# The first down product of a gated ConvFFN starts behind the last up product without a barrier between the two stages (fp32 two-layer backbone, one core)

## The reference, cut to what matters

```python
def conv_ffn(h, w_up, conv_w, conv_b, w_down):
    u = h @ w_up
    up = jnp.pad(u, ((0, 0), (1, 1), (0, 0)))
    u = up[:, :-2] * conv_w[0] + up[:, 1:-1] * conv_w[1] + up[:, 2:] * conv_w[2] + conv_b
    a, b = jnp.split(u, 2, axis=-1)
    return (jax.nn.gelu(a) * b) @ w_down

def post_add(x, y, g, gate):
    return x + gate * rms_norm(y, g)
```

## Time and profile before

| | |
|---|---|
| median of 3 runs | 1652.82 us |
| profiled execution, its own time | 1657.06 us |
| span of the profiled execution | 1655.3 us |
| PE busy in the span | 1518.8 us, 92% |
| DVE, ACT, POOL busy | 968.6, 728.8, 596.9 us |
| mean granted clock of PE | 0.97 |
| up stage's last product ends, down products start, layer 0 | 752.8, 760.1 us |
| the same, layer 1 | 1526.2, 1531.1 us |

### The profile page before, as it was taken

One profiled execution on the slowest core, in us unless ns is written; L12 is line 12 of the kernel. 1 busy time (PEld: TensorE's weight loads), 2 busy tenths in 40 slices (PEclk: granted clock), 3 DMA queues, 4 the chain that ended last, 5 costly groups with the idle time before them and its releaser, 6 DMA issues.

```text
span 1655.3 us, 22238 instructions
## 1 busy us (share of the span) xinstructions
PE 1518.8 (92%) x7560; PEld 1216.7 (74%) x7560; DVE 968.6 (59%) x1465; ACT 728.8 (44%) x1240; POOL 596.9 (36%) x529
## 2 busy tenths in 40 slices
PE   6889798889999999998999698889988899999998
PEld 1777466667888888886888577677776688887886
DVE  2448577557678666833334566688775544444455
ACT  3432466535323333323353445377774544443453
POOL 1342244233222222322333531364442444443454
PEclk9999799999999999999999899899999899999999
DMA  8120750104355344411122112010001233332232
GB/s 329 47 84 13 248 188 25 51 1 132 123 178 153 115 126 140 127 39 39 63 66 63 53 52 80 25 50 1 1 1 51 77 102 89 101 98 67 83 96 101
DMA packets 129135, 143.85 MB, mean 87 GB/s; under 512 B 7160, under 2 KB 95484, under 8 KB 129064
## 3 DMA queue, kind: packets, MB, share of 16 engines
q1 hardware_dynamic: 129064, 142.91, 27.6%
HBM read 140.79 MB, written 2.10 MB: 86 GB/s over the span
## 4 chain that ended last, share of the span: by engine, by line
PE 79%; DVE 8%; ACT 5%; POOL 3%; issue 2%; DMA 2%; SPq 0%; POOLq 0%; DVEq 0%; ACTq 0%
PE ps L462 22%; PE ps L463 22%; PE ps L464 22%; PE ps L1400 3%; PE ps L1386 2%; PE ps L1411 1%; ACT pT_hi L1451 1%; DVE hT_lo L781 1%; DVE hT_hi L779 1%; ACT prob L1440 1%; DMA start_w<-in_ada_w_dram 1%; PE ps L1413 1%; PE ps L666 1%; DVE o_tmp L1516 1%; DMA ada_w<-in_ada_w_dram 1%
## 5 line engine op out<-in xcount | busy, mean ns | idle before, releaser
L454 POOL TENSOR_TENSOR w_lo<-raw,w_hi 128x1024 fp32r<-128x1024 f32 (+1 forms) x184 | 348.0, 1893 | 644.9 <-ACT w_hi L447 644.9
L462 PE MATMUL ps<-hT_hi,w_hi 128*128 128x512 f32 (+1 forms) x1072 | 383.6, 358 | 7.3 <-DVE hT_lo L781 6.4
L463 PE MATMUL ps<-hT_lo,w_hi 128*128 128x512 f32 (+1 forms) x1072 | 381.2, 356 | 0.0
L464 PE MATMUL ps<-hT_hi,w_lo 128*128 128x512 f32 (+1 forms) x1072 | 378.8, 353 | 0.0
L447 ACT ACTIVATE w_hi<-raw 128x1024 fp32r<-128x1024 f32 (+1 forms) x200 | 172.9, 866 | 190.4 <-PE ps L464 166.6
L462 PEld LDWEIGHTS ps<-hT_hi,w_hi 128*128 128x128 f32 x1072 | 202.8, 189 | 46.6 <-DVE hT_lo L781 10.0
L464 PEld LDWEIGHTS ps<-hT_hi,w_lo 128*128 128x128 f32 x1072 | 202.0, 188 | 29.7
L463 PEld LDWEIGHTS ps<-hT_lo,w_hi 128*128 128x128 f32 x1072 | 202.7, 189 | 27.8
L2053 DVE TENSOR_TENSOR g_lo<-act_g,g_hi 128x768 fp32r<-128x768 f32 (+1 forms) x84 | 106.7, 1277 | 164.2 <-ACT g_hi L2003 162.9
L462 PE MATMUL ps<-w_hi,g_hi 128*128 128x512 f32 x420 | 166.0, 395 | 3.5 <-DVE g_lo L2053 3.0
L464 PE MATMUL ps<-w_hi,g_lo 128*128 128x512 f32 x420 | 164.0, 390 | 0.0
(11 more groups left out here) (234 smaller groups left out, 2497.0 us busy)
## 6 DMA issues: line engine op xcount, KB each, us to landing
raw<-in_ffn_w_up_dram SPq DMA_DIRECT2D x84, 512.0 KB, 3.9
ada_w_up<-in_ada_w_dram SPq DMA_DIRECT2D x48, 512.0 KB, 4.1
raw<-in_ffn_w_down_dram SPq DMA_DIRECT2D x84, 256.0 KB, 2.6
ada_w<-in_ada_w_dram SPq DMA_DIRECT2D x32, 512.0 KB, 5.0
start_w<-in_ada_w_dram SPq DMA_DIRECT2D x8, 1024.0 KB, 11.4
raw<-in_c_w_qkv_dram SPq DMA_DIRECT2D x12, 512.0 KB, 3.6
raw<-in_ab_w_in_dram SPq DMA_DIRECT2D x8, 512.0 KB, 4.1
raw<-in_ab_w_out_dram SPq DMA_DIRECT2D x8, 512.0 KB, 3.8
```

Source lines behind the costliest of these rows:

```text
L454: by.tensor_tensor(w_lo[:, slot, 0:width], raw[:, n % RAW, 0:width], w_hi[:, slot, 0:width].bitcast(F32), ALU.subtract).then_inc(lo_split, 1)
L462: nc.tensor.matmul(outp, s_hi, m_hi, start=first, stop=False, skip_group_check=True)
L463: nc.tensor.matmul(outp, s_hi, m_lo, start=False, stop=False, skip_group_check=True)
L464: return nc.tensor.matmul(outp, s_lo, m_hi, start=False, stop=last, skip_group_check=True)
```

## The change

The after_phase of the down stage goes from all four engines; the `close` of the up stage stays. The first activation tile is split into the unused fourth slot of `w_hi` and `w_lo` (`first_g`): ACT does it in the last turn behind unit 3, DVE's low part follows behind unit 4. ACT and DVE split tiles 1 and 2 where they split three before. PE's `gate_tensor` for the latent tokens follows the last up unit directly; the tiles of down unit 0 take their activations from the fourth slot, and before tile t of it PE waits for the taps of the up unit whose banks it overwrites (`TURNS * TURN + t // 2 + 1`). DVE's loop over the first half starts one turn later, since its first three are now written out. In layer 0 the condition of the copy into `gate_rows` is worded anew and takes place where it did.

```diff
@@ up_scalar, turn
                     else:
                         split_hi(act, f"down{l}", m - (TURN - 3), BANK, free=False)
+                    if last and m == 3:
+                        down_activation(act, l, nt, 0, 0, first=True)
...
             turn(TURNS - 1, True)
-            for m in range(3):
+            for m in (1, 2):
                 down_activation(act, l, nt, m, 0)
             close(act, "act")
@@ up_vector, turn
+                    if last and m == 4:
+                        down_remainder(dve, l, nt, 0, 0, 0, first=True)
@@ down_tensor
-            after_phase(pe, before)
             gate_tensor(pe, l, tag, 1, (0, 1))
...
+                    if first and not half:
+                        pe.wait_ge(s(f"taps{l}"), TURNS * TURN + t // 2 + 1)
                     tt = slice(t * P, (t + 1) * P)
-                    mm = mm3(bank(t), g_hi[:, slot, tt], g_lo[:, slot, tt], w_hi[:, slot, 0:BANK],
+                    gh, gl = first_g() if first and not half else (g_hi[:, slot, :], g_lo[:, slot, :])
+                    mm = mm3(bank(t), gh[:, tt], gl[:, tt], w_hi[:, slot, 0:BANK],
                              w_lo[:, slot, 0:BANK], first, last)
@@
+        def first_g():
+
+            return w_hi[:, 3, 0:TOK], w_lo[:, 3, 0:TOK]
+
-        def down_activation(act, l, nt, m, i):
+        def down_activation(act, l, nt, m, i, first=False):
             T = nt * P
-            nc.scalar.activation(g_hi[:, m, 0:T], act_g[:, bass.ds(i * 3 + m, 1), 0:T].rearrange("p a n -> p (a n)"),
+            g = first_g()[0] if first else g_hi[:, m, :]
+            nc.scalar.activation(g[:, 0:T], act_g[:, bass.ds(i * 3 + m, 1), 0:T].rearrange("p a n -> p (a n)"),
                                  ACT.Copy).then_inc(s(f"g_hi{l}"), 1)
@@ down_scalar, down_pool
-            after_phase(act, before)
...
-            after_phase(pool, before)
@@ down_vector
+        def down_remainder(dve, l, nt, half, m, i, first=False):
             T = nt * P
-            after_phase(dve, before)
+            dve.wait_ge(s(f"g_hi{l}"), i * 3 + (half * FT + m + 1))
+            gh, gl = first_g() if first else (g_hi[:, m, :], g_lo[:, m, :])
+            nc.vector.tensor_tensor(gl[:, 0:T], act_g[:, bass.ds(i * 3 + m, 1), 0:T].rearrange("p a n -> p (a n)"),
+                                    gh[:, 0:T].bitcast(F32), ALU.subtract).then_inc(s(f"g_lo{l}"), 1)
...
-            split_activations(0, 0, DTURNS)
+            for m in (1, 2):
+                down_remainder(dve, l, nt, 0, m, 0)
+            split_activations(0, 1, DTURNS)
```

More of the change, by code:

```diff
@@ L1893, in up_vector, with turn @@
             dve.sem_inc(s(f"taps{l}"), 3)
-            def turn(i, with_ada):
+            def turn(i, with_ada, last=False):
                 if with_ada:
@@ L1922, in turn @@
                                                 gelu[:, 0:T], conv_b[:, 0:T], ALU.mult).then_inc(s(f"gated{l}"), 1)
-                    if l == 0 and not with_ada and m == 1:
+                    if last and m == 4:
+                        down_remainder(dve, l, nt, 0, 0, 0, first=True)
+                    if l == 0 and last and m == 1:
                         dve.wait_ge(s("ada_sum"), 8)
@@ L1931, in up_vector @@
                 turn(i, l == 0)
-            turn(TURNS - 1, False)
+            turn(TURNS - 1, False, last=True)
             close(dve, "dve")
@@ L1946, in down_sync, with down_tensor @@
                         load_unit(sp, f"down{l}", half * FT + m, src, BANK, i, 3)
-        def down_tensor(pe, l, before, nt):
+        def down_tensor(pe, l, nt):
             phase, tag = f"down{l}", f"ffnpost{l}"
-            after_phase(pe, before)
             gate_tensor(pe, l, tag, 1, (0, 1))
@@ L1999, in down_split, with down_scalar @@
             down_activation(act, l, nt, m, i)
-        def down_activation(act, l, nt, m, i):
+        def first_g():
+            return w_hi[:, 3, 0:TOK], w_lo[:, 3, 0:TOK]
+        def down_activation(act, l, nt, m, i, first=False):
             T = nt * P
-            nc.scalar.activation(g_hi[:, m, 0:T], act_g[:, bass.ds(i * 3 + m, 1), 0:T].rearrange("p a n -> p (a n)"),
+            g = first_g()[0] if first else g_hi[:, m, :]
+            nc.scalar.activation(g[:, 0:T], act_g[:, bass.ds(i * 3 + m, 1), 0:T].rearrange("p a n -> p (a n)"),
                                  ACT.Copy).then_inc(s(f"g_hi{l}"), 1)
-        def down_scalar(act, l, before, nt):
+        def down_scalar(act, l, nt):
             tag = f"ffnpost{l}"
-            after_phase(act, before)
             for half in range(2):
@@ L2035, in down_scalar, with down_pool @@
             close(act, "act")
-        def down_pool(pool, l, before, nt):
-            after_phase(pool, before)
+        def down_pool(pool, l, nt):
             for half in range(2):
@@ L2044, in down_pool, with down_vector @@
             close(pool, "pool")
-        def down_vector(dve, l, before, nt):
+        def down_remainder(dve, l, nt, half, m, i, first=False):
             T = nt * P
-            after_phase(dve, before)
+            dve.wait_ge(s(f"g_hi{l}"), i * 3 + (half * FT + m + 1))
+            gh, gl = first_g() if first else (g_hi[:, m, :], g_lo[:, m, :])
+            nc.vector.tensor_tensor(gl[:, 0:T], act_g[:, bass.ds(i * 3 + m, 1), 0:T].rearrange("p a n -> p (a n)"),
+                                    gh[:, 0:T].bitcast(F32), ALU.subtract).then_inc(s(f"g_lo{l}"), 1)
+        def down_vector(dve, l, nt):
             def split_activations(half, first, last):
@@ L2051, in split_activations @@
                     for m in range(3):
[L2052 to L2055, removed]
-            split_activations(0, 0, DTURNS)
+                        down_remainder(dve, l, nt, half, m, i)
+            for m in (1, 2):
+                down_remainder(dve, l, nt, 0, m, 0)
+            split_activations(0, 1, DTURNS)
             if l == 0:
@@ L2112, in _ @@
                 up_tensor(pe, l, NT[l])
-                down_tensor(pe, l, b + 8, NT[l])
+                down_tensor(pe, l, NT[l])
         @block.scalar
@@ L2126, in _ @@
                 up_scalar(act, l, b + 7, NT[l])
-                down_scalar(act, l, b + 8, NT[l])
+                down_scalar(act, l, NT[l])
         @block.gpsimd
@@ L2140, in _ @@
                 up_pool(pool, l, b + 7)
-                down_pool(pool, l, b + 8, NT[l])
+                down_pool(pool, l, NT[l])
         @block.vector
@@ L2155, in _ @@
                 up_vector(dve, l, b + 7, NT[l])
-                down_vector(dve, l, b + 8, NT[l])
+                down_vector(dve, l, NT[l])
 def shape_constants():
```

## The result

| | before | changed |
|---|---|---|
| median of 6 runs each | 1652.27 us | 1643.63 us (1642.29 to 1647.71) |
| ratio, 95% interval | | 0.9947 (0.9930 to 0.9965) |
| profiled execution, its own time | 1657.06 us | 1647.71 us |
| step from up to down, layer 0 | 9.47 us | 2.12 us |
| step from up to down, layer 1 | 5.52 us | 2.12 us |

The forecast was 1642.3 us, the range 1639.8 to 1646.6.

The account below looks back on a forecast made before the run. PE, busy 92% of the span, was taken to bound the kernel. Savings of 7.25 (layer 0) and 3.28 (layer 1) sum to 10.53 us; 1652.82 - 10.53 = 1642.3 us, range 1639.8 to 1646.6.

Parts of the forecast that it names:

- PE's step bounds: Up to down, both layers: PE's waits for DVE's drain at the two barriers, 8.1 us in all, lengthen the kernel.
- What stays in the step: Between up and down products after the change: gates 1.72 us plus PE's drain 0.50, sum 2.22 per layer.
- The row of the drain between the halves: Profile row of PE's drain between the halves, used to price the drain left in the step at 0.50 us.
- Layer 0, 7.25 us: Layer 0's step from up to down costs 9.47 us; less the remaining 2.22, the saving is 7.25.
- Layer 1, 3.28 us: Layer 1's step from up to down costs 5.50 us; less the remaining 2.22, the saving is 3.28.
- The operands: First down units: weights, activations and taps arrive before PE needs them, so no stall enters the sum.
- the pessimistic ends: Unit 1's low part, latest start of DVE's subtraction: ready at least 0.41 us early in layer 0, 0.32 in layer 1.
- POOL in DVE's way: Unit 1: POOL's split or the drain delays DVE's subtraction in both layers; 2.6 us less saved, 1644.9; rival, 8%.
- given back: End of layer 0's stage: something paced by loads loses its share again, leaving 3.3 us saved, 1649.5; rival, 4%.
- ring without its lead: Down stages: each of 84 units would wait, at 5.8 us per unit costing some 17, time 1659; rival, 2%.
- stall that the barrier had covered: PE running from stage to stage without rest: idle 2.04 us once per layer, costing 4.1, so 1646.4; rival, 5%.

Follow-up runs that it names:

- two more subtractions: Changed kernel with two useless DVE subtractions between its last product and the low parts of tiles 1 and 2; median 1647.12 us, ratio 0.9961.

## Why the prediction was right

Steps of all ten traces, in us, with the time that each trace's execution took:

| kernel | step, layer 0 | step, layer 1 | between the steps | time |
|---|---|---|---|---|
| before | 9.47 | 5.52 | 763.9 | 1657.06 |
| before, second trace | 8.22 | 7.13 | 759.9 | 1650.13 |
| changed | 2.12 | 2.12 | 764.6 | 1647.71 |
| changed, second trace | 2.12 | 2.13 | 759.8 | 1643.47 |
| barrier in layer 0 | 9.49 | 2.11 | 764.5 | 1654.03 |
| barrier in layer 1 | 2.12 | 7.22 | 759.9 | 1644.63 |
| barrier on PE alone | 8.69 | 7.13 | 760.1 | 1651.89 |
| no early tile | 8.46 | 6.01 | 762.6 | 1654.39 |
| no drain on PE | 1.76 | 1.75 | 765.1 | 1643.70 |
| two more subtractions | 2.11 | 2.13 | 765.9 | 1647.38 |

- **PE's step bounds.** Right, and shown: with only PE held at the barrier the time is that of the kernel before; with the other engines held only where PE is held too, the layers' shares add.
- **What stays in the step.** Forecast 2.22 us, measured 2.12. The gates took 1.76 where I had 1.72, the drain 0.36 where I had 0.50 (the last from the kernel without it). The row of the drain between the halves was the right one to take; it was 0.14 too dear.
- **Layer 0, 7.25 us.** Measured 7.35 between the two first traces, 6.1 between the second ones, since the clock came back sooner in that trace of the kernel before. It fell in all four traces with a barrier here, and the step cost 8.2 to 9.5.
- **Layer 1, 3.28 us.** Measured 3.40 between the first traces and 5.0 between the second. This term was too small for three of the four traces with a barrier here: I took the granted clock of 1.00 behind the wait for the rule. In the three other traces it fell and the step cost 7.1 to 7.2. How often each happens, four traces don't say.
- **The operands.** Right that nothing waits. The margins were 0.70 and 0.61 us, of which DVE can use 0.57 and 0.47, and not the 0.41 and 0.32 of the pessimistic ends: the 0.60 us ahead of DVE's subtractions was nearly all barrier. DVE starts them 0.13 us behind its product, its drain included. The prediction's two ends were themselves 0.06 too large: it divided merged rows by three, 0.90 and 0.63, where one subtraction by itself takes 0.96 and 0.69.
- **POOL in DVE's way.** It was not, for units 1 and 2: POOL's split of unit 3 began at 760.48 in layer 0, behind both subtractions (757.91 + 1.83 = 759.74). In layer 1 the early tile did meet it, which the prediction had not looked at: POOL's split ran from 1516.20 to 1517.50, the early subtraction (shown above) began at 1517.09 and took 0.95 us, where the ones behind the step take 0.69, and ended 0.54 behind POOL's. DVE was idle behind it, so it cost nothing. In the steady ring a subtraction takes 1.31 us and ends 0.81 behind POOL's, and with two more subtractions one took 2.07. The rule of the Trainium skill's "SBUF — State Buffer" (Who interferes with whom) fits all of these.
- **Rivals.** The stretch from layer 1's first down product to the end is 123.7 us in both kernels' two traces each, and the windows show no new idle time. Layer 0's down stage, from the place of its first product at full clock to its last product, takes 176.2 to 176.3 us in both kernels' traces, so nothing is given back there either. There was no ring without its lead, and no stall that the barrier had covered (the rule of "Runtime: NRT & Kernel Launch", Instruction fetch mechanics, of the Trainium skill found no case that shows in these traces). The price of 17 us for the ring's rival was worked out wrongly: with three slots PE would wait once in three units and not at each, and in layer 0 two units take 36 x 0.227 = 8.2 us, so at 5.8 us only layer 1 would wait, 14 times. That is an estimate of 3 to 5 us, and the kernel would still have been faster than before.
- **Time.** From the profiled execution I had forecast 1646.5, and that execution took 1647.71; from the median 1642.3, and the medians are 1643.63 and 1643.42. The steps of the second pair of traces save 11.1 us, those of the first 10.75; the measured ratios give 8.8 (0.53% of 1652) and 10.8 (0.65% of 1654). The interval of each holds the forecast's 0.64%. That the sum holds for the second pair is luck in part: there layer 0 saved 1.15 less than forecast and layer 1 1.7 more.

## What to carry to other kernels

A barrier between two stages costs the engine that bounds them the whole tail of the slowest other engine; here it cost the clock behind it too, in seven of the eight waits traced. To gain anything, remove the wait and supply the first unit's operands early, in memory that the old stage no longer reads; here one of the two without the other gave nothing. Let the first unit be as long as the tail that it has to cover, and read the margin from the trace: here a conv, a product and one subtraction on DVE fitted behind the gates and 18 or 12 matmuls with half a microsecond to spare (the rows show 0.70 and 0.61 us, of which 0.57 and 0.47 proved usable).

## What the runs showed of the hardware

- The same wait of PE, 3.53 us between the same instructions, left the granted clock at 1.00 in one execution and was followed by 0.50 in another, with 1.6 us between the two. A wait of 2.08 us with gates just ahead was followed by a fall as well (0.63 in the window behind it), three matmuls into the new work. Behind the wait of 4.54 us the clock fell in four traces of four, but came back at different places, and the step cost 8.2 to 9.5 us. A single trace thus doesn't give the price of such a gap.
- A drain of PE amid dense work costs 0.36 us: 0.26 until the next matmul starts and 0.1 in the matmuls behind it.
- With the same instructions and the same busy time on the other engines, PE's mean granted clock differs by 0.01 from execution to execution, and the time by 4 to 5 us of 760. The difference lies where PE idles often (0.93 against 0.96 in the 357 to 361 us of norms and mixer); the dense stages take the same time to 0.1 us.
- A DVE subtraction of 768 columns with both inputs in SBUF took 0.95 us alone, 1.31 beside a POOL subtraction that began 0.8 us before it, and 2.07 when POOL began 0.04 before it. It ended 0.81 and 0.82 us behind POOL's in the two cases.
